# Key pages turned and PSUM zeroed between the projection's last sums, expert weights asked for after the token tiles

## What is computed

```python
z = rmsnorm(x) @ w_in            # 1024 -> 3072: q1 q2 k1 k2 va qb kb vb
# q, k rotated; new k, v returned
k_all = concat([cache_k_diff[page_table], k_new]); v_all = ...   # 2048 past keys per sequence, 16 pages of 128
oa = diff_core(q1, q2, k_all..., v_all..., lam)   # softmax - lam * softmax, times v
ob = merge_by_denominator([dilated_branch(...) for 3 patterns])
x = x + concat([rmsnorm(oa), ob]) @ w_out
x = x + hier_moe(rmsnorm(x))     # top group of 4, then top 2 of 8 experts: silu(x Wg) * (x Wu) @ Wd
# window caches are returned with 8 rows moved in: copies from cache to output
```

## Time and profile before

| | |
|---|---|
| median of 3 timed runs | 1969.51 us (1966.11 to 1974.11) |
| the profiled execution | 1967.08 us, span 1965.0 us |
| busy in the span | PE 83%, DVE 35%, ACT 17%, POOL 11% |
| chain that ended last | PE 48%, DMA 37%, DVE 9%, issue 3% |
| DMA | 659 MB moved, mean 335 GB/s |

### The profile page before, as it was taken

One profiled execution on the slowest core, in us unless ns is written; L12 is line 12 of the kernel. 1 busy time (PEld: TensorE's weight loads), 2 busy tenths in 40 slices (PEclk: granted clock), 3 DMA queues, 4 the chain that ended last, 5 costly groups with the idle time before them and its releaser, 6 DMA issues.

```text
span 1965.0 us, 32622 instructions
## 1 busy us (share of the span) xinstructions
PE 1636.5 (83%) x12772; PEld 777.4 (40%) x12772; DVE 695.6 (35%) x1351; ACT 331.4 (17%) x769; POOL 213.9 (11%) x356
## 2 busy tenths in 40 slices
PE   7999688888769787887778879998968788788884
PEld 3444355545425322332323347764442222323231
DVE  5455568867412500000000069984160000000005
ACT  3100244444302100000000020004120000000001
POOL 1000222322200100000000021000020000000000
PEclk9999789989889799899999989999979999989897
DMA  9994579989883799999999999704169999999995
GB/s 350 343 362 183 187 295 353 375 344 346 332 315 127 292 423 428 413 427 427 428 428 427 424 309 322 251 11 171 52 249 426 429 421 422 428 427 427 427 425 194
DMA packets 83829, 659.20 MB, mean 335 GB/s; under 512 B 15307, under 2 KB 15436, under 8 KB 45418
## 3 DMA queue, kind: packets, MB, share of 16 engines
q1 hardware_dynamic: 58906, 569.86, 72.8%
q0 software_dynamic: 24800, 87.65, 11.8%
HBM read 643.18 MB, written 96.53 MB: 376 GB/s over the span
## 4 chain that ended last, share of the span: by engine, by line
PE 48%; DMA 37%; DVE 9%; issue 3%; ACT 2%; SPq 1%; DVEq 0%; POOL 0%; ACTq 0%; POOLq 0%
DMA ring<-in 30%; PE ps L2285 14%; PE ps L2448 6%; PE ps L1865 6%; PE ps L2240 5%; PE ps L1831 3%; DMA x<-in 3%; PE ps L2054 2%; DVE ring L1283 2%; DMA ring<-y_rows 2%; PE ps L2469 2%; PE ps L2039 1%; DVE ring L1276 1%; PE ps L2305 1%; PE ps L1994 1%
## 5 line engine op out<-in xcount | busy, mean ns | idle before, releaser
L2285 PE MATMUL ps<-ring,big 128*32 128x512 f32 (+1 forms) x2688 | 478.6, 653 | 128.8 <-DMA ring<-in 122.8
L2285 PEld LDWEIGHTS ps<-ring,big 128*32 128x32 f32 (+1 forms) x2688 | 150.2, 132 | 452.9 <-issue 392.1
L1548 DVE TENSOR_TENSOR big<-big,ps 128x512 f32<-128x512 f32 x32 | 22.0, 687 | 822.0 <-PE ps L2285 775.7
L2305 PE MATMUL ps<-ring,big 128*32 128x512 f32 (+1 forms) x928 | 214.0, 602 | 17.1 <-ACT big L797 13.3
L797 ACT ACTIVATE big<-ps 128x512 f32<-128x512 f32 (+6 forms) x166 | 84.2, 516 | 829.3 <-PE ps L1831 531.7
L2240 PE MATMUL ps<-ring,big 128*128 128x512 f32 (+1 forms) x288 | 123.0, 609 | 5.7 <-ACT big L1191 4.8
L2448 PE MATMUL ps<-act_t,ring 128*128 128x288 f32 x512 | 124.4, 406 | 0.0
L2305 PE MATMUL ps<-act_t,big 128*32 128x512 f32 (+1 forms) x416 | 99.0, 594 | 14.1 <-ACT big L797 12.4
L2448 PEld LDWEIGHTS ps<-act_t,ring 128*128 128x128 f32 x512 | 97.2, 190 | 26.8
L1772 DVE SCALAR_TENSOR_TENSOR big<-big,par 128x512 f32<-128x512 f32 x240 | 103.9, 510 | 0.0
L1865 PE MATMUL ps<-ring,act_t 128*128 128x512 f32 x208 | 94.8, 604 | 6.2 <-DMA ring<-in 3.5
(11 more groups left out here) (322 smaller groups left out, 1793.4 us busy)
## 6 DMA issues: line engine op xcount, KB each, us to landing
ring<-in SPq DMA_DIRECT2D x180, 2048.0 KB, 18.7
out<-in SPq DMA_DIRECT2D x16, 4080.0 KB
ring<-in SPq DMA_DIRECT2D x128, 256.0 KB, 7.0
ring<-in POOLq DMA_DIRECT2D x128, 256.0 KB, 6.3
act_t<-in SPq DMA_DIRECT2D x16, 2048.0 KB
ring<-in SPq DMA_DIRECT2D x28, 1024.0 KB, 10.2
ring<-in SPq DMA_DIRECT2D x24, 512.0 KB
ring<-in POOLq DMA_DIRECT2D x24, 512.0 KB, 4.7
```

The source lines that it names most:

```text
L2285: ins = mm(ps[half, i, :], XgT[:, par_, k, half], slot(eslots(w)[i], 8)[:, k, :], start=(k == 0), stop=(k == KC - 1))
L2305: ins = mm(ps[half, 5 + h, :], hbT[:, k, half], down_weights(w, odd)[:, k, h * 512:(h + 1) * 512], start=(k == 0), stop=(k == 3))
```

## The change

Four edits, the first two on the side of the projection, the last two on SyncE.

1. In every chunk VectorE forms t3 before the sum u2_0 and t4 right after it, instead of after u4_0 and u2_1.
2. In chunk 2 the four `turn_pages` stand between the last sums, and the zeroing of banks 0, 1 and 7 between the last two; both are gone from after the loop and after the fence. For that the last two turns (k = 18 and 19) go to bank 5 instead of banks 0 and 1, with a wait for the sum c22_1, which reads bank 5, and turn 19 waits until turn 18 is copied out.
3. SyncE waits for `x_in` 32 before its first expert load (slot 5).
4. The two cache copies are written after slot 0's load instead of ahead of slot 2's wait; since 0 is followed by 2, this is the same place.

```diff
         for name in ("rows",) * (w == 0) + ("t1", "c11_0", "t2", "c11_1") + ("s4",) * (w == 2) + (
-                "u2_0", "u4_0", "t3", "c12_0", "u2_1", "t4", "u4_1", "c12_1", "u3_0", "c22_0", "u3_1", "c22_1", "c21_0", "c21_1"):
+                "t3", "u2_0", "t4", "u4_0", "c12_0", "u2_1", "u4_1", "c12_1", "u3_0", "c22_0", "u3_1", "c22_1", "c21_0", "c21_1"):
             Z_DVE[w, name] = 4 + len(Z_DVE) + 1
     Z_READY = 4 + len(Z_DVE)
+    Z_TURN_BANK = [k % 2 for k in range(18)] + [5, 5]
...
-                        if s == 2:
-                            for i in range(8, 10):
-                                copy_window(i)
                         sp.wait_ge(p_mm, (5, len(P_UNITS))[s - 2])
...
+                if l == 0 and s == 5:
+                    sp.wait_ge(x_in, 32)
                 expert_load(l, par_, par_, eslots(par_).index(s), None)
+                if l == 0 and s == 0:
+                    for i in range(8, 10):
+                        copy_window(i)
...
+            V.tensor_tensor(b12, b22, b12, ALU.subtract).then_inc(dve_ready, 1)
             dve.wait_ge(dve_ready, Z_DVE[w, "c11_0"])
             with_half("u2_0", 0, 5, "p6_0")
+            dve.wait_ge(dve_ready, Z_DVE[w, "t2"])
+            V.tensor_tensor(b21, b21, b11, ALU.subtract).then_inc(dve_ready, 1)
             z_sum(w, "u4_0", "p5_0", two_, 0, 6, half_sum[w][:, 0, :])
-            V.tensor_tensor(b12, b22, b12, ALU.subtract).then_inc(dve_ready, 1)
+            if w == 2:
+                turn_pages(0, 0)
...
             with_half("u2_1", 1, 4, "p6_1")
-            dve.wait_ge(dve_ready, Z_DVE[w, "t2"])
-            V.tensor_tensor(b21, b21, b11, ALU.subtract).then_inc(dve_ready, 1)
+            if w == 2:
+                turn_pages(0, 1)
...
             z_sum(w, "u4_1", "p5_1", two_, 1, 5, half_sum[w][:, 1, :])
+            if w == 2:
+                turn_pages(0, 2)
...
-            for i in range(2):
-                z_sum(w, f"c21_{i}", f"p4_{i}", one_, 2 + i, (4, 6)[i], half_sum[w][:, i, :])
+            z_sum(w, "c21_0", "p4_0", one_, 2, 4, half_sum[w][:, 0, :])
+            if w == 2:
+                turn_pages(0, 3)
+                dve.wait_ge(z_tev, 18)
+                S(V.memset(ps[:, 0:2, :], 0.0))
+                S(V.memset(ps[:, 7, :], 0.0))
+            z_sum(w, "c21_1", "p4_1", one_, 3, 6, half_sum[w][:, 1, :])
...
-        for k in range(4):
-            turn_pages(0, k)
         fence()
...
-        S(V.memset(ps[:, 0:2, :], 0.0))
-        S(V.memset(ps[:, 7, :], 0.0))
...
             if k > 1:
-                pe.wait_ge(z_tev, k - 1)
+                pe.wait_ge(z_tev, k if k == 19 else k - 1)
+            if k == 18:
+                pe.wait_ge(dve_ready, Z_DVE[2, "c22_1"])
```

More of the change, by code:

```diff
@@ L868, in z_turned @@
             act.wait_ge(z_tr, k + 1)
-            src = ps[:, k % 2, :].rearrange("p (h c) -> p h c", h=4)
+            src = ps[:, Z_TURN_BANK[k], :].rearrange("p (h c) -> p h c", h=4)
             w = n // 3
@@ L1856, in z_turn @@
             if k > 1:
-                pe.wait_ge(z_tev, k - 1)
+                pe.wait_ge(z_tev, k if k == 19 else k - 1)
+            if k == 18:
+                pe.wait_ge(dve_ready, Z_DVE[2, "c22_1"])
             for h in range(4):
-                ins = turn(ps[:, k % 2, h * P:h * P + r], zrow[0:r, k % 4, h * P:(h + 1) * P], r)
+                ins = turn(ps[:, Z_TURN_BANK[k], h * P:h * P + r], zrow[0:r, k % 4, h * P:(h + 1) * P], r)
             ins.then_inc(z_tr, 1)
```

## The result

The changed kernel takes 1951.23 us (median of 5, 1945.42 to 1956.57), the one before 1969.51 us; the ratio is 0.9908, 95% interval 0.9884 to 0.9932. It is faster, by 18.3 us where 28 were forecast from this median, and its time lies just above the predicted range. The profiled execution is the slowest of the five: 1956.57 us, span 1954.5.

What follows compares the result with a forecast made beforehand. TensorE was taken to stand still for VectorE before attention (11.30 us) and for late token tiles in the output projection (15.50 us). Gains 8.5 + 1.3 + 17.0 = 26.8 us gave 1940.3 or 1942.7, stated as 1941.5; range 1936 to 1951.

Steps and rivals of the forecast that it cites:

- Key pages and zeroing at nothing: Input projection: four transposes and two memsets moved between VectorE's sums were costed at nothing; 3.6 us if there were no idle.
- The fence: Before the attention stage: GpSimd, at 204.94, is late next, the fence costs 0.56 us, PE starts at 205.7; 8.5 us gained.
- GpSimd holds the fence: Rival, chance 0.12: GpSimd's drain waits for its transfers or its issues stretch; about 6 us gained there, 1944 to 1946.5.
- The clock after a shorter gap: Attention stage start: PE returns after 2.7 us, perhaps still at full clock; 0 to 2.6 us gained, 1.3 taken as the middle.
- Moved VectorE work and GpSimd's requests: Before the fence: VectorE's moved transposes do not slow GpSimd's eight page requests; the difference seen was 0.03 us.
- Expert weights after x: Output projection: with weights and copies requested after x, PE no longer waits before unit 4; 17.0 us gained.
- A later stage swallows part: Rival, chance 0.08: transfers pace the attention stage, so the first 9.8 us come to nothing; 1950 to 1952.
- x does not land sooner: Rival, chance 0.04: x's 42.92 us are its own, not the queue's, so PE waits as before; 1957 to 1960.
- VectorE held in mid-projection: Rival, chance 0.03: transpose 0 waits for key pages inside the sums and stops PE; 1984 if they came at 225.

## Why the prediction was right and wrong

**Key pages and zeroing at nothing: right.** The sums kept their pace and PE had no idle in the chunk. The projection ended at 206.7 in place of 203.0 because of something much earlier. PE's timeline between chunks 0 and 1 and the stretch behind it, each first before and then after:

```profile
93.95 0.66 PE L1831 MATMUL ps<-cst,x 128*128 128x128 f32 x4 [1.94 <-DVE x L1311]
94.72 1.11 PE L1841 MATMUL ps<-cst,x 128*128 128x128 f32 x4 [3.80 <-DVE x L1314]
```

```profile
95.00:100.00 5.00, 5.00 (x18) 1.78 (x18) 1.78 (x2) 0.24 (x1) 0.54 (x1) 1.00 0.81 295
95.00:100.00 5.00, 5.00 (x10) 2.42 (x10) 1.86 (x1) 0.60 (x1) 0.00 (x0) 0.50 0.86 303
```

PE is 0.8 us late there, and then runs at the lower clock until about 100.7, which accounts for the other 2.9. Two of the edits, t3 and t4, act in this chunk too, but the new order doesn't explain it: this stand was 1.7 to 3.5 us in the twelve other executions, and the kernel with the old order and SyncE's wait had 3.27, the clock at 0.50 from 95 to 100, and an end at 206.76. The ends spread from 202.2 to 206.8, with a mean of 204.5 in the old order and 204.4 in the new.

**The fence: the step that failed.** It is "What is late next is GpSimd, at 204.94. The fence costs 0.56 us as before". 204.94 is the end of GpSimd's last request, not of its arrival at the fence: its drain lasts until the DMA engines have done with the eight pages and 2.75 to 3.1 us more. Before, DMA's share of 0.82 from 206 to 208 puts the end of its work at about 207.6, so by my estimate the drain was over near 210.5, one and a half microseconds ahead of VectorE's 212.08: it was all but the bound already, and VectorE's 8.88 us hid it. The gain could be only that last piece, the 0.56 us of VectorE's own drain and the zeroing that no longer stands behind the fence: 207.6 + 2.9 + 0.4 = 210.9 in place of 214.29, so 3.4 us and not 8.5 (measured 3.3). With the drain taken out (stand 1.95) or its transfers moved behind the fence (1.39) the rest appears. The argument against the rival, "its idle after 204.94 is booked on VectorE's queue", was a misreading: a wait is booked on whoever ends last, and says nothing on when the others were done.

**The rival "GpSimd holds the fence" (0.12) is what happened**, by its mechanism. The gain that it left was put too high, at 5.5 to 6: it opened the fence when the transfers ended (208), and left out the 2.9 us between that and the drain's end. With 3.3 the sum is 17.0 + 3.3 = 20.3, 1949.2 us against the median before; measured 1951.2, and 1950 and 1949.6 by the other two ratios.

**The clock after a shorter gap (1.3 us): nothing came of it, and the question behind it was not tested by the change, since the gap stayed long.** Where it was short, the clock fell anyway after a stand of 1.95 us (twice) and held after 1.39 us (twice). The Trainium skill (TensorE: Matmul & The Clock Gate, Part 1), as cited in the prediction, says that the fall doesn't follow the kernel's own start; in twelve executions it came 2.2 to 5.4 us after the last work of the projection, which agrees. No run has a gap of 2.7 us; taking the middle had no better ground than either end.

**Moved VectorE work and GpSimd's requests: right.** Eight took 4.59 us with a transposition and the zeroing beside them, and 4.55 without. GpSimd did hold the fence, but not by slower requests.

**Expert weights after x: right** in each row: x after 9.9 us, no idle, 7.09 us, 16.9 of 17.0 us, and no later wait for weights; alone it gave 0.9899 and 0.9909.

**A later stage swallows part (0.08): not seen where it could be told.** 9.4 us more of stand cost 11, and 6.0 us less gave 5.8. For the 3.3 us of the projection's edits it stays open: the timings give 1.3, with as much uncertainty, and no profile shows a place where the rest is lost. **x does not land sooner** and **VectorE held in mid-projection**: refuted by the same rows. The range ended 0.2 us below the measured time because the fence rival was put at 1944 to 1946.5 where it belonged at 1949; with the same 3 us for the spread it would have reached 1952.

## What to carry to other kernels

An engine reaches a fence when its drain ends, not when its last instruction does; on GpSimd, with transfers under way, the drain took 5.4 to 6.5 us. Before moving work off the engine that a fence waits for, work out when each of the others would arrive, transfers included, and let an idle time that is booked on one engine prove nothing about the rest. If requests stand ahead of a fence only to be early, try them behind it: here that was worth 12.9 us by the medians, more than the projection's edits had given, and with all of them the kernel is 1.7% faster than before.

## What the runs showed of the hardware

GpSimd's drain behind its own DMA requests lasted until the 16 DMA engines had gone idle plus 2.75 to 3.1 us, in six executions (2.88, 2.85, 2.83, 2.75, 3.08, 2.79), whatever the number of requests (four or eight pages of 256 KB). The Trainium skill (DMA: Bandwidth & Descriptors, section "Anatomy of one DMA — SWDGE (gpsimd) path") puts most of a fixed cost of about 2 us per transfer on confirming the last write; the pause here is some 0.8 to 1.1 us longer than that, and no run shows what it is made of.

The clock can fall after PE has come back: with a stand of 1.95 us it fell 1.0 and 0.6 us into the new work, and full clock returned at 210.5 and 210.3, 3.4 us later. After 1.39 us it did not fall there.
